# Hybrid decoder trunk: coefficient buffers moved by 960 bytes, the convolution norm's last gate ahead of its spread, two tiles and the squares of x made over the layer's end, gathers one a tile

## The chip, the cores and the metric

One core of one Trainium2 chip runs the whole program, two layers on 512 tokens, in one launch. The metric is the device time in microseconds.

## The reference, cut to what matters

```python
for l in range(DEPTH):                                   # DEPTH = 2, D = 1024, 512 tokens, fp32
    mod = silu(c) @ ada_w[l] + ada_b[l]
    sh1, sc1, g1, sh2, sc2, g2 = split(mod, 6)
    h = rms_norm(x, norm_mix_g[l]) * (1 + sc1) + sh1
    q, k, v, glu, gates = split(h @ w_in[l])             # 16 query heads, 4 key heads of 64
    attn = sliding_window_attention(rope(q), rope(k), v, sinks) @ w_o_attn
    u = ga * sigmoid(gb)
    u = silu(layer_norm(causal_conv31(u), conv_ln_g, conv_ln_b))
    merged = sigmoid(g_attn) * attn + sigmoid(g_conv) * (u @ w_o_conv)
    x = x + g1 * (merged @ w_out)
    h = rms_norm(x, norm_ffn_g[l]) * (1 + sc2) + sh2
    s = product_key_scores(h @ w_query, sub_keys)        # 8 heads, 2 x 128 keys
    ids, gate = top 16 of the pairs of the two halves' top 16, softmax
    x = x + g2 * sum(gate * gelu(u_tab[ids] . h) * v_tab[ids])
```

## The kernel before, in words

Every product with a weight matrix goes over a stream of tiles of 128 x 1024 numbers (512 KB), NT = 340 a layer: 28 input projections (4 glu, 2 keys, 2 values, 8 queries, 12 glu), attention gates and outputs (28 to 43), convolution gates 44 to 47 (I_CG), convolution outputs from 48, w_out at 60, queries of the retrieval at 68, then 128 tiles of the table u (I_U = 84) and 128 of the table v (I_W = 212). SP loads tile n into one of four slots of `raw` once tile n - 4 is used up; ACT rounds it to fp32r (`high`, L850), and DVE or POOL subtracts to get the low part in place (`w_low`, L1212; `u_low`, L1610; `weight_low`, L1672; POOL's `low`, L488). PE then makes 24 products a tile: high by high, high by low, low by high, over eight chunks of 128 features (`product`, L546 to L548; two tiles together in `first_pair`, L560 to L562; table v in `experts`, L804 to L806). Each engine's order is written out by hand, with counting semaphores between.

**A norm** (`norm`, twice a layer): ACT squares a chunk of x into one of two `sq` buffers (L880), PE adds over the features with four small products a chunk (`token_sums`, L578), ACT takes the root, DVE the inverse and a diagonal matrix (L1218, L1221), PE spreads it over the partitions (`spread`, L586), and DVE, ACT and DVE make each chunk of h, in high and low parts. The convolution's norm goes in the same way, with silu instead (L1041). There `spread` comes ahead of gate tile I_CG + 3, and ACT reads that gate out of its bank (`first_gate(3)`, L1015) only behind its eight silus; the first pair of the convolution's outputs needs that bank.

**The start.** SP issues the small inputs, ACT x and 16 rows of ada_w, then ACT makes silu of c and two sines of which DVE makes the arguments; DVE multiplies the rows with it (L1178). Tiles 0 and 1 are loaded, rounded by ACT at the head of a layer, and their low parts made by POOL.

**Retrieval.** Table u is multiplied densely for the last 384 tokens; for the first 128 POOL gathers rows (L507), one for each of 128 chosen experts of 128 tokens, into four slots, and DVE takes their dot product with h (`dot`, L1496); a slot is refilled once its dot is done (L519 to L523). While PE takes tiles 0 to 35 of u, DVE makes the top-k of the 4 token blocks, alone on its engine (L1533 to L1604), POOL makes the low parts, and ACT stops for one exp a block (`EXP_TILES`, L1095). From tile 36 (`U_ROUTE`) on DVE makes the low parts; between tiles 38 and 39 PE transposes the routing. From tile 40 on DVE makes one-hot matrices for 48 groups of 8 tokens (L1632, L1635), PE multiplies them (L778), and dots are shared out over the groups (`DOTS_BY_GROUP`); after the last group each of the last ten low parts has a dot behind it (L1640), then come any dots that are left (L1644). Table v starts with two `mix` (L1659) of what the first table left in memory (`cg`), a weight's low part and `mixed_low` (L1666); each tile's coefficients stand in `cf_hi` and `cf_lo`, four buffers each. DVE adds the gathered rows of v beside them (`weigh`, L1651).

At the layer's end DVE adds eight chunks to x (L1728) as PE transposes the sparse part (L812); after the last layer SP stores each chunk.

## Time and profile before

| | us |
|---|---|
| three runs | 3776.2, 3789.8, 3793.5; median 3789.8 |
| the profiled execution, its own time | 3782.4 |
| its span, first to last instruction | 3780.6 |
| PE busy | 3615.9 (96%) |
| DVE busy | 3099.5 (82%) |
| ACT busy | 1574.4 (42%) |
| POOL busy | 1381.1 (37%) |

The profile is one execution recorded by the hardware. PE is the matrix engine, DVE the vector engine, ACT the scalar engine, POOL GpSimd, SP the queue that issues most transfers. L12 is line 12 of the kernel before. A row of a timeline is: start in us from the span's start, duration in us, engine, line, operation, what it writes and reads, count, and in brackets how long the engine had been idle before it and what ended that. PE's instructions overlap, so a busy PE is not one at its best pace. An fp32 product stands as two instructions.

### The profile page before, as it was taken

The page shows a single profiled execution, that of the slowest core. Times are in us where ns is not written, and L with a number is a line of the kernel's source. Part 1 is how long each engine was busy: PE and PEld are TensorE (multiplying, and loading weights), DVE is VectorE, ACT ScalarE, POOL GpSimd, SP SyncE. Part 2 cuts the span into 40 slices and gives each one's busy share as a digit, 9 for nine tenths or more (in the row PEclk, how much of TensorE's full clock was granted, in tenths as well). Part 3 has the DMA queues.
Part 4 walks back from the last instruction along what each step waited for, and adds up shares of the span by engine and source line. Part 5 has one row for each costly group of instructions (what it writes and reads, how often), then busy time and mean ns, then how long its engine had stood idle before and what let it go on. Part 6 is the DMA issues. An engine that isn't in the chain of part 4 may idle for free.

```text
span 3780.6 us, 61655 instructions
## 1 busy us (share of the span) xinstructions
PE 3615.9 (96%) x19426; PEld 3325.2 (88%) x19426; DVE 3099.5 (82%) x6295; ACT 1574.4 (42%) x2321; POOL 1381.1 (37%) x1136
## 2 busy tenths in 40 slices
PE   5999899999999999999999998999999999999999
PEld 4766678989999999999987676889999999999999
DVE  6799765997888978888868995669978888788888
ACT  3474324434444533333345633244444554333332
POOL 0000002463555645454400000035645555545555
PEclk9999899999999999999999998989999999999999
DMA  4111253456999999999921111724579999999998
GB/s 178 62 56 56 67 215 119 133 175 204 317 335 346 289 350 342 339 339 342 330 87 62 51 67 58 255 95 140 177 228 331 356 322 301 353 333 345 350 336 283
DMA packets 408317, 862.51 MB, mean 228 GB/s; under 512 B 165488, under 2 KB 231024, under 8 KB 407664
## 3 DMA queue, kind: packets, MB, share of 16 engines
q1 hardware_dynamic: 294720, 528.08, 41.8%
q0 software_dynamic: 73728, 268.47, 20.2%
q10 hardware_dynamic: 39600, 62.93, 4.4%
q8 instruction: 100, 1.64, 0.2%
q14 instruction: 169, 1.38, 0.1%
HBM read 773.36 MB, written 85.98 MB: 227 GB/s over the span
## 4 chain that ended last, share of the span: by engine, by line
issue 47%; PE 34%; POOL 11%; DVE 4%; DMA 3%; ACT 0%; POOLq 0%; SPq 0%; DVEq 0%; ACTq 0%
PE ps L804 9%; PE ps L806 9%; PE ps L805 9%; POOL w_lo L488 7%; POOL gbuf L507 3%; PE ps L548 2%; PE ps L546 2%; PE ps L547 2%; POOL spare L522 2%; DMA raw<-stream 2%; PE ps L778 1%; DVE oneR L1635 1%; DVE gbuf L1496 1%; DVE oneL L1632 1%; DMA gbuf<-u_rows,ids_u 1%
## 5 line engine op out<-in xcount | busy, mean ns | idle before, releaser
L850 ACT CAST w_hi<-raw 128x1024 fp32r<-128x1024 f32 x680 | 715.3, 1055 | 910.7 <-DMA raw<-stream 864.2
L546 PE MATMUL ps<-h_hi,w_hi 128*128 128x384 f32 (+1 forms) x2944 | 1069.7, 363 | 25.6 <-POOL w_lo L488 16.3
L547 PE MATMUL ps<-h_lo,w_hi 128*128 128x384 f32 (+1 forms) x2944 | 1042.9, 354 | 0.0
L548 PE MATMUL ps<-h_hi,w_lo 128*128 128x384 f32 (+1 forms) x2944 | 1042.3, 354 | 0.0
L804 PE MATMUL ps<-cf_hi,w_hi 128*128 128x384 f32 x2048 | 697.2, 340 | 9.3 <-DVE cf_lo L1666 4.8
L806 PE MATMUL ps<-cf_hi,w_lo 128*128 128x384 f32 x2048 | 691.7, 338 | 0.0
L805 PE MATMUL ps<-cf_lo,w_hi 128*128 128x384 f32 x2048 | 687.1, 336 | 0.0
L522 POOL TENSOR_TENSOR spare<-spare 128x1 f32<-128x1 f32 x504 | 339.3, 673 | 901.5 <-DVE y_sp L1651 474.3
L546 PEld LDWEIGHTS ps<-h_hi,w_hi 128*128 128x128 f32 x2944 | 560.0, 190 | 79.2 <-POOL w_lo L488 18.1
L547 PEld LDWEIGHTS ps<-h_lo,w_hi 128*128 128x128 f32 x2944 | 559.8, 190 | 38.7 <-issue 5.8
L548 PEld LDWEIGHTS ps<-h_hi,w_lo 128*128 128x128 f32 x2944 | 558.8, 190 | 37.0
L488 POOL TENSOR_TENSOR w_lo<-raw,w_hi 128x1024 fp32r<-128x1024 f32 x108 | 288.6, 2678 | 332.3 <-ACT w_hi L850 332.0
L804 PEld LDWEIGHTS ps<-cf_hi,w_hi 128*128 128x128 f32 x2048 | 384.5, 188 | 12.3 <-DVE w_lo L1672 9.1
L507 POOL DMA_INDIRECT gbuf<-stream,ids_v x256 | 379.9, 1484 | 38.2 <-POOL spare L522 2.7
L507 POOL DMA_INDIRECT gbuf<-u_rows,ids_u x256 | 370.8, 1448 | 40.1 <-POOL spare L522 7.5
L805 PEld LDWEIGHTS ps<-cf_lo,w_hi 128*128 128x128 f32 x2048 | 384.5, 188 | 0.0
L806 PEld LDWEIGHTS ps<-cf_hi,w_lo 128*128 128x128 f32 x2048 | 383.9, 187 | 0.0
L499 POOL TENSOR_TENSOR spare<-spare 128x1 f32<-128x1 f32 x2 | 0.4, 193 | 1032.9 <-DVE w_lo L1212 1032.9
L1651 DVE SCALAR_TENSOR_TENSOR y_sp<-gbuf,a_sp,y_sp 128x1024 f32<-128x1024 f32 x256 | 327.1, 1278 | 5.2 <-DMA gbuf<-stream,ids_v 5.2
L1090 ACT ACTIVATE g_out<-ps 128x384 f32<-128x384 f32 x256 | 125.6, 491 | 490.9 <-PE ps L548 490.7
L1303 DVE SCALAR_TENSOR_TENSOR yT<-uT,lp,yT 128x512 f32<-128x512 f32 x480 | 327.6, 745 | 0.1
L1496 DVE CUSTOM_DVE_ANT_1 gbuf<-gbuf,h_tok 128x1024 f32<-128x1024 f32 x256 | 303.2, 1220 | 25.1 <-DMA gbuf<-u_rows,ids_u 25.0
(232 smaller groups left out, 4980.1 us busy)
## 6 DMA issues: line engine op xcount, KB each, us to landing
raw<-stream SPq DMA_DIRECT2D x680, 512.0 KB, 4.6
gelu_scratch<-g_out ACTq DMA_DIRECT2D x256, 192.0 KB
cg<-gelu_scratch SPq DMA_DIRECT2D x256, 192.0 KB, 5.9
c_scratch<-stage SPq DMA_DIRECT2D x64, 512.0 KB, 8.4
cg<-c_scratch SPq DMA_DIRECT2D x256, 128.0 KB, 4.9
qT<-ada SPq DMA_DIRECT2D x32, 512.0 KB, 6.0
cgate<-ada SPq DMA_DIRECT2D x32, 512.0 KB, 5.3
w_rows<-ada SPq DMA_DIRECT2D x32, 512.0 KB, 7.4
```

Source lines behind the costliest of these rows:

```text
L488: nc.gpsimd.tensor_tensor(w_lo[:, s], raw[:, s], w_hi[:, s].bitcast(F32), ALU.subtract).then_inc(lo_done, 1)
L507: nc.gpsimd.indirect_dma_start(out=gbuf[:, n % SLOTS], out_offset=None, in_=table, in_offset=bass.IndirectOffsetOnAxis(ap=ids[:, k:k + 1], ...
L522: nc.gpsimd.tensor_tensor(spare[:, 16:17], spare[:, 17:18], spare[:, 18:19], ALU.add).then_inc(room, 1)
L546: nc.tensor.matmul(ps[:, b, 0:n], wh, hi[:, c, t0:T], start=c == 0, stop=False)
L547: nc.tensor.matmul(ps[:, b, 0:n], wh, lo[:, c, t0:T], start=False, stop=False)
L548: mm = nc.tensor.matmul(ps[:, b, 0:n], wl, hi[:, c, t0:T], start=False, stop=c == C - 1)
L804: nc.tensor.matmul(ps[:, c, P:T], w_hi[:, s, c], cf_hi[s][:], start=first, stop=False)
L805: nc.tensor.matmul(ps[:, c, P:T], w_hi[:, s, c], cf_lo[s][:], start=False, stop=False)
L806: mm = nc.tensor.matmul(ps[:, c, P:T], w_lo[:, s, c], cf_hi[s][:], start=False, stop=last)
L850: nc.scalar.copy(w_hi[:, s], raw[:, s]).then_inc(hi_done, 1)
L1303: ins = nc.vector.scalar_tensor_tensor(out=yT[:, c], in0=uT[:, c, k:k + T], scalar=weight, in1=yT[:, c], op0=ALU.mult, op1=ALU.add)
L1496: nc.vector.tensor_tensor_reduce(out=row, in0=row, in1=h_tok[:, :, 0:P], scale=1.0, scalar=0.0, op0=ALU.mult, op1=ALU.add, accum_out=a_sp[ ...
```

## The change

- The buffers from `rstd` on begin 960 bytes later, and `cf_lo2` and `cf_lo3` are moved inside the space of h's low part. Widths stay.
- The squares of x for the mixer's norm get eight buffers of their own (over sq, hx, hs, sg). They and the rounding of the next layer's first two tiles come at the end of a layer, and ahead of the loop for layer 0. DVE adds the squares of chunks 4 to 7 into one, so that PE sums five sets and not eight, and DVE, not POOL, makes the low parts of tiles 0 and 1. The stream gets two more tiles at its end, for loads with no reader.
- SP issues x, the rows of ada and tiles 0 and 1 at the start.
- The convolution's gate tile I_CG + 3 is multiplied ahead of the spread; ACT copies its bank to `cgate` at once and takes the sigmoid there behind the silus.
- The exps come at tiles 8, 16, 24, 33; POOL's first four gathers come one a tile from tile 16; six dots come ahead of the routing's copies, and 104 are shared out over the groups.

Three new semaphores for the squares and one for the gate are left out below, as is unchanged code.

```diff
--- before.py
+++ after.py
@@ -47,9 +47,9 @@
...
 PART = NKEYS // PARTS
-EXP_TILES = (6, 14, 23, 32)
+EXP_TILES = (8, 16, 24, 33)
 SLOTS = 4
-GATHER_TILE = 18
+GATHER_TILE = 16
@@ -57,7 +57,7 @@
...
 ROW4 = PAIRS[1][0] * TOPK // 4 - PAIRS[1][0]
-DOTS_BY_GROUP = 118
+DOTS_FIRST, DOTS_BY_GROUP = 6, 104
@@ -202,6 +202,7 @@
...
         sinT = keep("sinT", [P, T])
+        cur[0] += 960
@@ -276,12 +277,13 @@
...
         cf_lo = [at("cf_lo0", rstd_base, [P, ND], F32R), at("cf_lo1", base + 67 * KB, [P, ND], F32R),
-                 at("cf_lo2", h_lo_base + 4 * KB, [P, ND], F32R), at("cf_lo3", h_lo_base + 6 * KB, [P, ND], F32R)]
+                 at("cf_lo2", h_lo_base + 4928, [P, ND], F32R), at("cf_lo3", h_lo_base + 6464, [P, ND], F32R)]
...
         gbuf = at("gbuf", sq_base, [P, SLOTS, D])
+        x_squares = at("x_squares", sq_base, [P, C, T])
@@ -399,7 +405,12 @@
...
             sp.dma_start(cact[:], c_d.broadcast_to([P, D])).then_inc(c_in, 16)
+            sp.dma_start(xT[:], x_d).then_inc(x_in, 16)
             sp.dma_start(params[:], params_d).then_inc(const_in, 16)
+            for n in range(ADA_1):
+                if n >= 12 and n % 2 == 0:
+                    sp.dma_start(raw[:, n // 2 - 6], stream[n // 2 - 6]).then_inc(loaded[n // 2 - 6], 16)
+                sp.dma_start(rows0[:, n], ada[n]).then_inc(ada_in[n // 4], 16)
@@ -421,7 +432,9 @@
...
-                with sp.Fori(0, 52 // 4) as r:
+                load(2, l * NT + 2)
+                load(3, l * NT + 3)
+                with sp.Fori(1, 52 // 4) as r:
@@ -469,6 +482,8 @@
...
                 w_loads(3, 0, 28, False)
+                load(0, l * NT + NT)
+                load(1, l * NT + NT + 1)
@@ -480,6 +495,7 @@
...
             nc.gpsimd.memset(spare[:, 15:20], 0.0).then_inc(lo_done, 4)
+            pool.wait_ge(lo_done, 4)
@@ -488,9 +504,6 @@
...
-                pool.wait_ge(lo_done, l * NT + 4)
-                for i in range(2):
-                    low(i, l * NT + i)
@@ -513,9 +526,8 @@
...
                     low(u % 4, l * NT + I_U + u)
-                    if u == GATHER_TILE:
-                        for n in range(SLOTS):
-                            gather(n)
+                    if GATHER_TILE <= u < GATHER_TILE + SLOTS:
+                        gather(u - GATHER_TILE)
@@ -572,11 +584,11 @@
...
-                def token_sums(b, c):
+                def token_sums(b, squares, first, last):
                     for tt in range(NB):
-                        mm = nc.tensor.matmul(ps[:, b, 2 * tt:2 * tt + 2], sq[:, c % 2, tt * P:(tt + 1) * P],
-                                              mean[:, 0:2], start=c + tt == 0, stop=c == C - 1 and tt == NB - 1)
+                        mm = nc.tensor.matmul(ps[:, b, 2 * tt:2 * tt + 2], squares[:, tt * P:(tt + 1) * P],
+                                              mean[:, 0:2], start=first and tt == 0, stop=last and tt == NB - 1)
@@ -587,13 +599,14 @@
...
-                def norm_sums(w):
-                    for c in range(C):
-                        pe.wait_ge(sq_done, (2 * l + w) * C + c + 1)
-                        token_sums(7 * w, c).then_inc(sq_used, 1)
-                    spread(7 - w, 3 * l + 2 * w)
-                norm_sums(0)
+                for c in range(5):
+                    if c < 4:
+                        pe.wait_ge(sqx_done, l * C + c + 1)
+                    else:
+                        pe.wait_ge(sqx_sum, 3 * l + 3)
+                    mm = token_sums(0, x_squares[:, c], c == 0, c == 4)
+                mm.then_inc(sqx_used, 1)
+                spread(7, 3 * l)
@@ -719,10 +732,9 @@
...
                     pe.wait_ge(ln_sq, l * C + c + 1)
-                    token_sums(6, c).then_inc(ln_mm, 1)
+                    token_sums(6, sq[:, c % 2], c == 0, c == C - 1).then_inc(ln_mm, 1)
+                proj(I_CG + 3, h_hi, h_lo)
                 spread(5, 3 * l + 1)
-                for i in range(I_CG + 3, I_CG + FIRST_GATES):
-                    proj(i, h_hi, h_lo)
@@ -730,7 +742,10 @@
...
                 proj_loop(I_OUT + 4, I_QRY, o_hi, o_lo)
-                norm_sums(1)
+                for c in range(C):
+                    pe.wait_ge(sq_done, l * C + c + 1)
+                    token_sums(7, sq[:, c % 2], c == 0, c == C - 1).then_inc(sq_used, 1)
+                spread(6, 3 * l + 2)
@@ -829,9 +844,6 @@
...
-            act.dma_start(xT[:], x_d).then_inc(x_in, 16)
-            for n in range(ADA_1):
-                act.dma_start(rows0[:, n], ada[n]).then_inc(ada_in[n // 4], 16)
@@ -839,8 +851,22 @@
...
             nc.scalar.copy(ident_r[:], ident).then_inc(id_r, 1)
+            def root_table():
+                nc.scalar.activation(spare[:, 30:31], eps, ACT.Sqrt)
+            def squares_of_x(c):
+                nc.scalar.activation(x_squares[:, c], xT[:, c], ACT.Square).then_inc(sqx_done, 1)
+            root_table()
+            act.wait_ge(x_in, 16)
+            for c in range(C):
+                squares_of_x(c)
             act.wait_ge(primed, 1)
-            act.wait_ge(x_in, 16)
+            for i in range(2):
+                act.wait_ge(loaded[i], 16)
+                nc.scalar.copy(w_hi[:, i], raw[:, i]).then_inc(hi_done, 1)
@@ -858,28 +884,13 @@
...
-                def root_table():
-                    nc.scalar.activation(spare[:, 30:31], eps, ACT.Sqrt)
...
-                def norm(w):
-                    root_table()
-                    for c in range(C):
-                        n = (2 * l + w) * C + c
-                        if w == 0:
-                            act.wait_ge(x_upd, l * C + c + 1)
-                        else:
-                            act.wait_ge(bank_read[c % 2], read_no(I_OUT + c))
-                        if c >= 2:
-                            act.wait_ge(sq_used, (2 * l + w) * C + c - 1)
-                        nc.scalar.activation(sq[:, c % 2], xT[:, c], ACT.Square).then_inc(sq_done, 1)
-                    act.wait_ge(sq_used, (2 * l + w) * C + C)
-                    token_root(7 * w)
+                def modulated(w):
@@ -891,9 +902,9 @@
...
-                high_at(0)
-                high_at(1)
-                norm(0)
+                act.wait_ge(sqx_used, l + 1)
+                token_root(0)
+                modulated(0)
@@ -1034,6 +1045,8 @@
...
                 token_root(6)
+                act.wait_ge(tile_done, l * NT + I_CG + 3 + 5)
+                nc.scalar.copy(cgate[:, 3], ps[:, 1]).then_inc(bank_read[1], 1)
@@ -1042,7 +1055,8 @@
...
                     nc.scalar.copy(n_hi[:, c], hs[:, c % 2]).then_inc(ln_hi, 1)
-                first_gate(3)
+                act.wait_ge(bank_read[1], read_no(I_CG + 3))
+                nc.scalar.activation(cgate[:, 3], cgate[:, 3], ACT.Sigmoid).then_inc(late_gate, 1)
@@ -1059,7 +1073,15 @@
...
                         act.dma_start(keys[:], keys_d[ll]).then_inc(key_in, 16)
-                norm(1)
+                root_table()
+                for c in range(C):
+                    act.wait_ge(bank_read[c % 2], read_no(I_OUT + c))
+                    if c >= 2:
+                        act.wait_ge(sq_used, l * C + c - 1)
+                    nc.scalar.activation(sq[:, c % 2], xT[:, c], ACT.Square).then_inc(sq_done, 1)
+                act.wait_ge(sq_used, (l + 1) * C)
+                token_root(7)
+                modulated(1)
@@ -1139,6 +1161,12 @@
...
                         high_at(I_W + NKEYS - 4 + s + 2)
+                high_at(NT)
+                root_table()
+                for c in range(C):
+                    act.wait_ge(x_upd, (l + 1) * C + c + 1)
+                    squares_of_x(c)
+                high_at(NT + 1)
@@ -1185,11 +1213,28 @@
...
             parameters(slice(0, 1))
+            def sum_squares(counted):
+                dve.wait_ge(sqx_done, (counted + 1) * C)
+                nc.vector.tensor_tensor(x_squares[:, 4], x_squares[:, 4], x_squares[:, 5], ALU.add).then_inc(sqx_sum, 1)
+                nc.vector.tensor_tensor(x_squares[:, 6], x_squares[:, 6], x_squares[:, 7], ALU.add).then_inc(sqx_sum, 1)
+                dve.wait_ge(sqx_sum, 3 * counted + 2)
+                nc.vector.tensor_tensor(x_squares[:, 4], x_squares[:, 4], x_squares[:, 6], ALU.add).then_inc(sqx_sum, 1)
+            def first_low(i):
+                dve.wait_ge(hi_done, i + 1)
+                nc.vector.tensor_tensor(w_lo[:, i], raw[:, i], w_hi[:, i].bitcast(F32), ALU.subtract).then_inc(lo_done, 1)
...
                 modulate(rows0[:, n], mv[:, C + n:C + n + 1])
+                if n == 7:
+                    sum_squares(0)
+                if n >= ADA_1 - 2:
+                    first_low(n - ADA_1 + 2)
@@ -1346,7 +1391,6 @@
...
-                dve.wait_ge(lo_done, l * NT + 2 + 4)
@@ -1432,6 +1476,8 @@
...
                         dve.wait_ge(bank_read[m % 2], read_no(I_CG + m))
+                        if m == 3:
+                            dve.wait_ge(late_gate, l + 1)
@@ -1616,6 +1662,8 @@
...
                 dve.wait_ge(h_ev, 2 * l + 2)
+                for _ in range(DOTS_FIRST):
+                    dot()
@@ -1635,7 +1683,7 @@
...
                     last_one.then_inc(lr_done, 1)
-                    while dots[0] < (g + 1) * DOTS_BY_GROUP // GROUPS:
+                    while dots[0] < DOTS_FIRST + (g + 1) * DOTS_BY_GROUP // GROUPS:
@@ -1722,12 +1770,14 @@
...
                 prepare(l + 1)
+                w_low(NT)
...
                                                    in1=xT[:, c], op0=ALU.mult, op1=ALU.add).then_inc(x_upd, 1)
-                dve.wait_ge(x_upd, (l + 2) * C)
+                sum_squares(l + 1)
+                w_low(NT + 1)
@@ -1761,7 +1811,7 @@
...
                   a["peer_v"][l].reshape(P, NKEYS, C, P).transpose(1, 0, 2, 3)]
-    stream = np.concatenate(tiles)
+    stream = np.concatenate(tiles + [tiles[0][:2]])
```

## Rows read from the trace of the kernel before

**Rows 1.** The page: engines over the whole span.

```profile
PE 3615.9 (96%) x19426; PEld 3325.2 (88%) x19426; DVE 3099.5 (82%) x6295; ACT 1574.4 (42%) x2321; POOL 1381.1 (37%) x1136
```

**Rows 2.** Groups by line, PE: busy us, mean ns | idle us before, releasers.

```profile
L778 PE MATMUL ps<-oneR,oneL 128*128 128x128 f32 x1536 | 190.1, 277 | 17.0 <-DVE oneR L1635 16.8
```

**Rows 3.** Timeline of the start: ACT, DVE and PE.

```profile
23.92 1.06 ACT L836 ACTIVATE cact<-cact 128x1024 f32<-128x1024 f32 x1
...
30.15 1.22 DVE L1178 CUSTOM_DVE_ANT_0 rows<-rows,cact 128x1024 f32<-128x1024 f32 x1
...
53.36 0.20 DVE L1218 RECIPROCAL rs<-rs 128x8 f32<-128x8 f32 x1
...
59.17 0.77 PE L560 MATMUL ps<-h_hi,w_hi 128*128 128x512 f32 x1 [3.15 <-DVE h_lo L1230]
```

**Rows 4.** Transfers from 0 to 60 us, in 40 slices of 1.5 us.

```profile
GB/s 0 177 287 365 340 422 361 418 422 415 424 418 421 418 423 421 415 421 426 415 423 412 426 415 366 19 0 0 0 0 0 0 0 0 0 0 0 0 5 0
DMA packets 3602, 14.21 MB, mean 237 GB/s; under 512 B 400, under 2 KB 400, under 8 KB 3472
```

**Rows 5.** Timeline at the two layer ends: PE and DVE.

```profile
1912.14 11.00 PE L578 MATMUL ps<-con,sq 128*128 128x2 f32 x64 [0.98 <-issue]
...
3772.54 5.36 DVE L1728 SCALAR_TENSOR_TENSOR xT<-ps,md,xT 128x512 f32<-128x512 f32 x8 [1.43 <-PE ps L812]
```

**Rows 6.** Timeline of PE at the convolution's norm and the second norm.

```profile
446.79 9.77 PE L578 MATMUL ps<-con,sq 128*128 128x2 f32 x48 [1.04 <-ACT sq L1021]
...
473.86 0.76 PE L560 MATMUL ps<-n_hi,w_hi 128*128 128x512 f32 x1 [8.01 <-ACT cgate L1015]
...
487.63 0.49 PE L546 MATMUL ps<-n_hi,w_hi 128*128 128x512 f32 x1 [0.35 <-DVE hx L1445]
...
604.88 0.80 PE L560 MATMUL ps<-h_hi,w_hi 128*128 128x512 f32 x1 [3.06 <-DVE h_lo L1230]
...
617.48 1.16 PE L743 MATMUL ps<-keys,qk 128*128 128x128 f32 x8
```

**Rows 7.** Timeline of the routing: PE, DVE and POOL.

```profile
779.94 0.44 PE L546 MATMUL ps<-h_hi,w_hi 128*128 128x384 f32 x1 [2.79 <-POOL w_lo L488]
...
796.43 7.43 DVE L1600 TENSOR_TENSOR routed<-t,esum 128x128 f32<-128x128 f32 x1
...
796.70 7.00 POOL L488 TENSOR_TENSOR w_lo<-raw,w_hi 128x1024 fp32r<-128x1024 f32 x3
...
799.11 0.69 PE L546 MATMUL ps<-h_hi,w_hi 128*128 128x384 f32 x1 [5.92 <-POOL w_lo L488]
...
873.74 0.44 PE L546 MATMUL ps<-h_hi,w_hi 128*128 128x384 f32 x1 [2.09 <-DVE w_lo L1610]
...
888.50 1.49 DVE L1621 COPY ijg<-ps 128x384 f32<-128x384 f32 x3 [12.54 <-PE ps L790]
```

**Rows 8.** Stretch of tiles 0-35: PE, PEld, DVE, ACT, POOL, clock, DMA, GB/s.

```profile
710.00:872.00 162.00, 152.94 (x869) 151.47 (x868) 158.50 (x457) 68.61 (x87) 103.11 (x38) 0.98 0.55 169
```

**Rows 9.** Timeline from the last dot to the second table: DVE and PE.

```profile
1355.43 1.22 DVE L1496 CUSTOM_DVE_ANT_1 gbuf<-gbuf,h_tok 128x1024 f32<-128x1024 f32 x1
...
1364.14 0.42 DVE L1659 TENSOR_TENSOR coef<-cg 128x256 f32<-128x256 f32 x1 [4.68 <-DMA cg<-gelu_scratch]
...
1366.51 0.44 PE L804 MATMUL ps<-cf_hi,w_hi 128*128 128x384 f32 x1 [2.50 <-DVE cf_lo L1666]
```

**Rows 10.** DMA issues, 1318 to 1364 us: count, median us to landing.

```profile
gbuf<-u_rows,ids_u POOLq DMA_INDIRECT x9, 7.8
```

**Rows 11.** Stretches, PE alone: length, busy (count), clock, DMA share, GB/s.

```profile
1400.00:1640.00 240.00, 240.00 (x1368) 1.00 1.00 346
711.00:769.00 58.00, 58.00 (x336) 1.00 0.55 162
...
79.00:95.00 16.00, 16.00 (x72) 1.00 0.29 99
347.00:368.00 21.00, 21.00 (x92) 1.00 0.24 76
```

4 lines of the change are left out of this document (added).

## The prediction, before the change was run

> **What bounds the kernel now.** The page's engine table comes first: TensorE (PE) is busy for 96% of the span, so time can only come from PE's remaining idle time and from the pace at which its instructions follow one another [rows 1]. Next, the groups by line for PE with the idle time before each, both layers summed: among them 17.0 us before the one-hot products, waiting for DVE [rows 2]. Then the timelines around those places, read for what ended each wait; last the starts of PE's instructions, to see their spacing. Times below are of layer 0; layer 1 repeats the pattern, and I double.
>
> **The start.** ACT issues x and 16 rows of ada itself, its queue fills up, and so its first activation runs only at 23.92 us, and with it silu, both tables, DVE's row products and PE's first real product, at 59.17, come late [rows 3]. The transfers are not what it waits for at the end: 14.21 MB move at about 420 GB/s and are done by 37.5 us [rows 4]. The change puts all issues on SP, in the order pos, constants, c, x, parameters, rows, with two tiles put between the last rows. Ahead of the last row then stand 13.1 of those 14.2 MB, which lands it near 36 us; SP's issues are 22 in a row, and nothing else waits on that queue but tiles 2 and 3, wanted after 50 us. ACT no longer issues, so silu and both tables are through by about 18 us, before the first four rows are in (about 18.6). DVE then does 16 products of 1.2 us, now with 2 us of added sums and two low parts that POOL had made, of the same 128 x 1024 elements and so 1.2 us each. The last group of four rows decides: 36 + 4 x 1.2 + 2.4 = 43.2 us, where DVE's reciprocal stood at 53.36. From it to PE's first product everything stays (59.17 - 53.36 = 5.8 us), so PE starts at 49 and not at 59. **-10 us** (bounds -6, if the single queue drains as slowly as in its first 5 us, and -12).
>
> **Between the layers.** The last tile's x updates run 5.36 us on DVE (the row is layer 1's), then the token sums hold PE for 11.00 us from 1912.14: eight sets, 1.4 us each on average [rows 5]. After the change there are five sets. ACT squares each chunk behind DVE's update (0.67 us a piece), with nothing to wait for, and is done at about 1912.8; DVE's three additions of 0.7 us end at 1915; PE is still in its first four sets then, so the fifth finds its data. Five average sets would take 6.9 us; the first ones, straight behind busy PE work, should be the quick ones, so I take 5.5 instead of 11.0: **-5.5 us** (bounds -4 and -7). The two weight tiles made here cost nothing: DVE stands still before the first update, and the second tile lies beside PE's sums; without that cover they would cost 1.2 us each. POOL loses this work and nobody waits for it. Once only, at the very end of the program, the same squares, sums and low part run with no reader: DVE ends some 4 us after its last update (3772.54 + 5.36 = 3777.9), the last output landed 2.7 us after it, with the span's end, **+1 us**.
>
> **The last convolution gate.** Before, PE's sums end at 456.6, then come spread, gate tile 3 (to 465.9), and an idle wait of 8.01 us for a bank that ACT frees only after its whole silu chain; the first pair is through at 487.6 [rows 6]. After, the tile runs straight behind the sums (24 products at 0.23 us and the first of them at the lower clock, to about 464), ACT copies the bank out, spread takes 1.2 us (four fp32 products at full clock, as the row of L743), and the first pair follows chunk by chunk as in the second norm: 3.06 us of wait and 12.6 us of work [rows 6]. End at about 481: 6.6 us earlier. What is late next is the weight tile behind the pair: its high part stands on ACT behind silus and the moved sigmoid with its table load, so I give back 0.6. **-12 us** for two layers (bounds -8 and -15). The DVE wait added for that sigmoid comes four tiles later and costs nothing.
>
> **Routing, gathers one a tile.** PE loses 2.79 us where ACT waits for the second exp, and 5.92 us where POOL issues four gathers in a row; both go, since exp comes two tiles later, and one gather fits beside one low part in the 4.16 us of a tile (24 products at 173.6 ns). But PE cannot keep this: at tile 36 the low parts pass to DVE, which comes there only when its routing chain ends, and PE waits for it already today, 2.09 us, to 873.74 [rows 7]. That chain is DVE's alone: DVE is busy for 158.50 us of the 162 up to there [rows 8]. So of the 8.7 us only what the chain itself gets shorter is kept. It loses 7.1 us in one place, an operation of 0.29 us that took 7.43 behind three low parts which POOL made up in a row after its gathers; spread out, these parts of 2.3 us will hold up other operations instead [rows 7]. I take 4 us kept: **-8 us** for two layers (bounds -17 and +9, the latter if the 7.1 us stay in another form and two more operations a layer are held up).
>
> **Dots.** Six dots move into DVE's 12.54 us wait for the transposes [rows 7], where they are free: the first four find their rows, two wait for a refill and end about 2 us before the wait does. The groups then carry 104 instead of 118. Of 17 us before the one-hot products [rows 2] I take **-6 us** (bounds 0 and -12). But 6 + 104 + 10 (one with each remaining low part) is 120: eight dots stay over, and they stand behind the last low part, ahead of the first coefficients. Today the last dot ends at 1356.6, DVE's second mix starts at 1364.14, when its data has landed, and PE starts the second table at 1366.5 [rows 9]. Eight dots on four slots are two rounds; a gather lands 7.8 us (median) after its issue in this stretch [rows 10], so they end near 1371 to 1373, and the mix follows. **+16 us** for two layers (bounds 0, if rows land fast, and +26).
>
> **Addresses.** The 960 bytes and the two offsets move all eight coefficient buffers, and with them o and n, to 448 modulo 512 (by the allocation's sums; now cf_hi, cf_lo0, cf_lo1, o and n stand at 0, cf_lo2 and cf_lo3 at 128, h at 128). Four stretches in which PE never waits give the spacing of its instructions, each as the stretch plus one instruction's own length over their count [rows 11]: coefficients, 384 columns, 240.34 / 1368 = 175.7 ns; h, 384 columns, 58.33 / 336 = 173.6; h, 512 columns, 16.4 / 72 = 227.8; o, 512 columns, 21.4 / 92 = 232.5. So streams that start at 0 are slower than those at 128, by 2.1 and 4.7 ns. No row shows 448. Bounds: downward the pace of h (2.1 x 6144 + 4.7 x 1152 = 18 us less), upward the coefficients as far above h as o is (2.6 x 6144 = 16 us more). I take the pace of h, because 0 is the only start seen slow, and all eight buffers leave it: **-18 us**. The Trainium skill, page "SBUF — State Buffer", section "SBUF: two separate sides", says that TensorE has ports of its own and waits for nobody, so an address would change nothing: by it this term is 0 and the sum 18 us higher. The two paces speak against it, if nothing but the address parts them. It is the first rival.
>
> **The sum.** -10 - 5.5 + 1 - 12 - 8 - 6 + 16 - 18 = -42.5. The profiled execution took 3782.4 us (span 3780.6): 3740. It is below the median of the three runs shown (3789.8); the mean of all four is 3785.5, so I add 3: **3743 us**.
>
> **Rivals.**
> 1. **The address gives nothing.** For it: the weights' loads and the moving data share an engine, and 448 is seen nowhere; against it: the two paces in the rows. 3743 + 18 = 3761 us. Chance 0.24.
> 2. **The leftover dots cost nothing,** because their rows have landed and the second mix waits for cg in any case (1364.14). Against it: a refill needs the dot before. 3743 - 16 = 3727 us. Chance 0.08.
> 3. **They cost double,** with the first weigh waiting for v rows whose gathers stand behind the eight dots: 3759 us. Chance 0.05.
> 4. **Slower: POOL's parts and gathers stretch the routing chain.** Its 36 low parts a layer now come evenly, while DVE is in two-input operations; if half of them hold up operations that go free today, at 2.3 us each, the chain grows by 42 us a layer, all of it paid at tile 36: 3743 + 8 + 84 = 3835 us. It decides from some 13 such hits a layer (3809 us). Against it: half of the chain is single-input searches, which lose nothing. Chance 0.05.
>
> The forecast itself has 0.58. **The numbers.** A measurement of this kernel tells about 0.5% (19 us) from no change. Forecast: 0.56 faster, 0.02 same; rival 1: 0.17 and 0.07; rival 2: 0.08 faster; rival 3: 0.04 and 0.01; rival 4: 0.01 same, 0.04 slower. Together 0.85, 0.11 and 0.04. The range 3722 to 3768 holds rivals 1 to 3 and the forecast with its bounds of 10 to 15 us.
>
> **What would show it.** First product of PE near 49 us. Token sums between the layers x40 in about 5.5 us. No wait on L1015's gate; a 3 us wait before the first pair instead. The two idle times of 2.79 and 5.92 gone, and that before tile 36 up from 2.09 to 6 or 7 us. PE's wait before the second table up from 2.50 to about 10 us, with eight dots behind the last low part. Coefficient products 173.5 ns apart. The forecast is wrong if that spacing stays, if tile 36 starts later against the second norm than now, or if the wait at the second table stays under 4 us.

## The result, and the profile after

The changed kernel takes 3750.0 us (median of 4 runs, 3743.4 to 3753.8), the kernel before 3785.7 beside it on the same chip (4 runs, 3776.2 to 3793.5): ratio 0.9905, 95% interval 0.9875 to 0.9934, that is 36 us or 0.95% less. The profiled run has a span of 3741.6 us against 3780.6.

The page's engine row of the changed kernel (before: [rows 1]):

```profile
PE 3580.1 (96%) x19378; PEld 3297.4 (88%) x19378; DVE 3098.4 (83%) x6310; ACT 1577.9 (42%) x2333; POOL 1390.0 (37%) x1132
```

PE has 48 instructions less (three sets of sums, twice), and 36 us less of busy time. The groups by line on PE show where its waits went (busy, mean ns | idle before, releasers; both layers):

```profile
L558 PE MATMUL ps<-h_hi,w_hi 128*128 128x384 f32 (+1 forms) x2944 | 1067.7, 363 | 21.4 <-DVE w_lo L1656 16.7 <-POOL w_lo L504 4.5
L819 PE MATMUL ps<-cf_hi,w_hi 128*128 128x384 f32 x2048 | 692.2, 338 | 38.0 <-DVE cf_lo L1714 29.4 <-DVE w_lo L1720 8.4
L793 PE MATMUL ps<-oneR,oneL 128*128 128x128 f32 x1536 | 187.9, 275 | 2.1 <-DVE oneR L1683 2.1
```

The coefficient products in the kernel before:

```profile
L804 PE MATMUL ps<-cf_hi,w_hi 128*128 128x384 f32 x2048 | 697.2, 340 | 9.3 <-DVE cf_lo L1666 4.8 <-DVE w_lo L1672 4.5
```

The wait before the one-hot products, 17.0 us before [rows 2], is 2.1; in its place the coefficient products wait 38.0 us and not 9.3, 29.4 of them for the first coefficient's low part of each layer. L558 was L546 before, L572 was L560, L819 was L804, L793 was L778.

The same in stages, from start to start of PE's instructions (us, layer 0 / layer 1; each is the difference of two start times in the timelines; a spread is the group of products by which PE copies a norm's factors over the partitions):

| stage | before | after | change, both |
|---|---|---|---|
| start, to the first spread | 53.9 | 44.4 | -9.5 |
| first norm's spread to second norm's | 545.8 / 543.4 | 538.5 / 537.7 | -13.0 |
| to table u's first product (queries) | 110.6 / 111.9 | 111.9 / 110.7 | +0.1 |
| to tile 40 (routing) | 186.8 / 187.5 | 180.2 / 182.6 | -11.5 |
| to tile 117 (groups) | 420.9 / 418.3 | 409.4 / 408.8 | -21.0 |
| to the second table's first product | 48.5 / 48.3 | 60.5 / 61.0 | +24.7 |
| second table | 544.2 / 543.0 | 539.9 / 541.1 | -6.2 |
| layer 0's end, to the next spread | 13.3 | 9.6 | -3.7 |
| last product to the span's end | 4.1 | 5.5 | +1.4 |

Together -38.7, the spans' difference but for rounding.

**Start.** Timeline of the changed kernel, ACT, DVE, PE:

```profile
7.33 1.06 ACT L848 ACTIVATE cact<-cact 128x1024 f32<-128x1024 f32 x1 [5.29 <-DMA cact<-c_in]
...
18.39 1.23 DVE L1206 CUSTOM_DVE_ANT_0 rows<-rows,cact 128x1024 f32<-128x1024 f32 x1 [1.50 <-DMA rows<-ada]
...
43.83 0.20 DVE L1263 RECIPROCAL rs<-rs 128x8 f32<-128x8 f32 x1
...
49.49 0.79 PE L572 MATMUL ps<-h_hi,w_hi 128*128 128x512 f32 x1 [3.00 <-DVE h_lo L1275]
```

Silu runs at 7.33 instead of 23.92 and the row products start at 18.39, when their rows land; the reciprocal is 9.5 us earlier, and so is all behind it [rows 3].

**Gate.** PE at the convolution's norm:

```profile
435.91 9.67 PE L590 MATMUL ps<-con,sq 128*128 128x2 f32 x48 [1.04 <-ACT sq L1032]
445.44 0.77 PE L558 MATMUL ps<-h_hi,w_hi 128*128 128x512 f32 x1
...
453.34 1.05 PE L598 MATMUL ps<-rstd,con 128*128 128x128 f32 x8
457.77 0.76 PE L572 MATMUL ps<-n_hi,w_hi 128*128 128x512 f32 x1 [3.38 <-DVE n_lo L1462]
...
471.62 0.50 PE L558 MATMUL ps<-n_hi,w_hi 128*128 128x512 f32 x1 [1.28 <-DVE hx L1491]
```

From the sums after their wait to the tile behind the pair it is 35.71 us (471.62 - 435.91), before 40.84 (487.63 - 446.79 [rows 6]). The 8.01 us wait for ACT's bank is gone; 3.38 us stand in its place, and 1.28 (2.43 in layer 1) behind the pair, where it had been 0.35. In layer 1 the same stretch takes 35.46 us, before 40.84: 10.5 us in both layers.

**Routing.** PE before tile 36 in both layers, and the one place where POOL still holds it up:

```profile
780.77 0.45 PE L558 MATMUL ps<-h_hi,w_hi 128*128 128x384 f32 x1 [2.23 <-POOL w_lo L504]
...
853.25 0.69 PE L558 MATMUL ps<-h_hi,w_hi 128*128 128x384 f32 x1 [4.08 <-DVE w_lo L1656]
...
2703.73 0.69 PE L558 MATMUL ps<-h_hi,w_hi 128*128 128x384 f32 x1 [8.22 <-DVE w_lo L1656]
```

2.79 and 5.92 [rows 7] have become 2.23 and nothing, and the wait for DVE's routing chain (the top-k work that it has to end before it makes low parts) has grown from 2.09 to 4.08 in layer 0 and 8.22 in layer 1.

**From the first table to the second.** DVE, then PE:

```profile
1326.42 1.23 DVE L1542 CUSTOM_DVE_ANT_1 gbuf<-gbuf,h_tok 128x1024 f32<-128x1024 f32 x1 [1.81 <-DMA gbuf<-u_rows,ids_u]
...
1331.70 1.22 DVE L1542 CUSTOM_DVE_ANT_1 gbuf<-gbuf,h_tok 128x1024 f32<-128x1024 f32 x1 [4.04 <-DMA gbuf<-u_rows,ids_u]
...
1340.76 1.22 DVE L1542 CUSTOM_DVE_ANT_1 gbuf<-gbuf,h_tok 128x1024 f32<-128x1024 f32 x1 [1.77 <-DMA gbuf<-u_rows,ids_u]
...
1341.91 0.42 DVE L1707 TENSOR_TENSOR coef<-cg 128x256 f32<-128x256 f32 x1
...
1344.81 0.68 PE L819 MATMUL ps<-cf_hi,w_hi 128*128 128x384 f32 x1 [14.46 <-DVE cf_lo L1714]
```

The eight leftover dots end at 1341.9; six of them wait for the row of a slot that was refilled only after an earlier dot, three of which are shown. The mix then starts without a wait (before, it waited for cg [rows 9]). PE's wait is 14.46 us, where it was 2.50.

**Layer end.** Five sets of sums, where there were eight [rows 5]:

```profile
1885.96 7.38 PE L590 MATMUL ps<-con,x_squares 128*128 128x2 f32 x40 [0.83 <-ACT x_squares L860]
```

### The profile page after: what moved, and what is told of

It is laid out like the page before. It is cut to its first block, busy times and chain, and to the rows that moved or that the text cites. A ratio compares the mean times of both kernels' runs of the same rounds, so it can differ in the third digit from the quotient of the medians.

```text
span 3741.6 us, 61584 instructions
## 1 busy us (share of the span) xinstructions
PE 3580.1 (96%) x19378; PEld 3297.4 (88%) x19378; DVE 3098.4 (83%) x6310; ACT 1577.9 (42%) x2333; POOL 1390.0 (37%) x1132
## 4 chain that ended last, share of the span: by engine, by line
PE 40%; issue 35%; DVE 11%; POOL 10%; DMA 2%; ACT 2%; POOLq 0%; DVEq 0%; SPq 0%; ACTq 0%
PE ps L819 9%; PE ps L820 8%; PE ps L821 8%; POOL gbuf L520 4%; PE ps L558 4%; PE ps L560 4%; PE ps L559 4%; POOL w_lo L504 3%; POOL spare L534 3%; DMA raw<-stream 1%; DVE yT L1348 1%; PE ps L793 1%; DVE i L1554 1%; DVE eq L1625 1%; PE ps L590 1%
## 5 line engine op out<-in xcount | busy, mean ns | idle before, releaser
L558 PE MATMUL ps<-h_hi,w_hi 128*128 128x384 f32 (+1 forms) x2944 | 1067.7, 363 | 21.4 <-DVE w_lo L1656 16.7
L560 PE MATMUL ps<-h_hi,w_lo 128*128 128x384 f32 (+1 forms) x2944 | 1041.3, 354 | 0.0
L819 PE MATMUL ps<-cf_hi,w_hi 128*128 128x384 f32 x2048 | 692.2, 338 | 38.0 <-DVE cf_lo L1714 29.4
L534 POOL TENSOR_TENSOR spare<-spare 128x1 f32<-128x1 f32 x504 | 359.9, 714 | 884.3 <-DVE a_sp L1542 442.3
L558 PEld LDWEIGHTS ps<-h_hi,w_hi 128*128 128x128 f32 x2944 | 558.4, 190 | 74.4 <-DVE w_lo L1656 17.8
L560 PEld LDWEIGHTS ps<-h_hi,w_lo 128*128 128x128 f32 x2944 | 557.0, 189 | 38.2
L819 PEld LDWEIGHTS ps<-cf_hi,w_hi 128*128 128x128 f32 x2048 | 386.1, 189 | 42.6 <-DVE w_lo L1720 42.1
L512 POOL TENSOR_TENSOR spare<-spare 128x1 f32<-128x1 f32 x2 | 0.4, 192 | 1022.7 <-DVE w_lo L1257 1022.7
L520 POOL DMA_INDIRECT gbuf<-u_rows,ids_u x256 | 358.0, 1398 | 39.1 <-POOL spare L534 9.9
```

Source lines behind the costliest of these rows:

```text
L520: nc.gpsimd.indirect_dma_start(out=gbuf[:, n % SLOTS], out_offset=None, in_=table, in_offset=bass.IndirectOffsetOnAxis(ap=ids[:, k:k + 1], ...
L534: nc.gpsimd.tensor_tensor(spare[:, 16:17], spare[:, 17:18], spare[:, 18:19], ALU.add).then_inc(room, 1)
L558: nc.tensor.matmul(ps[:, b, 0:n], wh, hi[:, c, t0:T], start=c == 0, stop=False)
L560: mm = nc.tensor.matmul(ps[:, b, 0:n], wl, hi[:, c, t0:T], start=False, stop=c == C - 1)
L819: nc.tensor.matmul(ps[:, c, P:T], w_hi[:, s, c], cf_hi[s][:], start=first, stop=False)
```

## The experiments

Medians stand beside the kernel before, run on the same chip in the same hour (3783.2 to 3785.6); "against the changed kernel" compares with its 3750.0, which was measured at another time, so that a difference of some 3 us says nothing. The ratios of experiments 1, 2 and 12 and of the 256 bytes in 5 have intervals clear of the changed kernel's (0.9875 to 0.9934); the others overlap it, and there the stages of the one profiled execution have to carry the reading. Every run but the second is an edit of the changed kernel.

**1 and 2. The addresses, taken back, and alone.**

```diff
-        cur[0] += 960
...
-                 at("cf_lo2", h_lo_base + 4928, [P, ND], F32R), at("cf_lo3", h_lo_base + 6464, [P, ND], F32R)]
+                 at("cf_lo2", h_lo_base + 4 * KB, [P, ND], F32R), at("cf_lo3", h_lo_base + 6 * KB, [P, ND], F32R)]
```

The second run is the kernel before with the opposite of this and nothing else.

> The changed kernel with the 960 bytes and the two offsets taken back (coefficient buffers, o and n again at 0, two low parts at 128, modulo 512). Theory (the start address sets the pace of the products): coefficient products go from 173.0 back to about 175.4 ns apart, o's and n's to 232, while the waits inside the second table, which grew when the pace rose, shrink again by some 5 us a layer; net about +8 us against the changed kernel, near 3758. As the prediction had it: +18, 3768. Rival (the pace came from something else in the change): spacing stays at 173.0, time stays at 3750.

> The kernel before with only the 960 bytes and the two offsets. Theory (the start address sets the pace, but part of what it gives is lost in waits for low parts of the weights inside the second table): spacing 173.0 ns for coefficients, second table about 540 to 541 us long instead of 544, and -6 to -8 us in all, near 3778. As the prediction had it: -18, 3768. Rival (the pace came from something else in the change): spacing 175.4, time 3786.

Measured: taken back 3767.6 us (5 runs, 3764.8 to 3771.6; ratio to before 0.9955, interval 0.994 to 0.9969), alone 3767.9 us (8 runs, 3757.8 to 3780.0; ratio 0.9957, 0.994 to 0.9974). The address is worth 17.6 us from the one side (3767.6 - 3750.0) and 17.3 from the other (3785.2 - 3767.9). Stretches of 200 us in the second table and of 40 us with o, in which PE never waits: the changed kernel, then the kernel with the addresses back (columns as in [rows 8]):

```profile
1400.00:1600.00 200.00, 200.00 (x1156) 200.00 (x1155) 168.74 (x253) 69.25 (x96) 104.06 (x95) 1.00 1.02 351
528.00:568.00 40.00, 40.00 (x176) 32.81 (x176) 28.37 (x44) 11.46 (x13) 5.01 (x3) 1.00 0.81 303
```

```profile
1400.00:1600.00 200.00, 200.00 (x1140) 200.00 (x1139) 167.70 (x250) 68.97 (x95) 109.90 (x100) 1.00 1.01 344
530.00:570.00 40.00, 40.00 (x173) 32.15 (x173) 28.21 (x44) 11.47 (x13) 5.00 (x3) 1.00 0.81 297
```

Worked as in the prediction, 200.34 / 1156 = 173.3 ns against 200.34 / 1140 = 175.7, at the same clock and the same DMA load. The kernel with the addresses alone has x1156 in 200 us, too. My own expectation, +8 and -7, was half of what came. I had taken the 6.2 us of the second table's row for the whole; but the changed kernel loses more in waits inside that table, whatever the addresses: what the intervals of over 0.2 us between its products have beyond 173.5 ns adds up, over both layers, to 7.4 us before, 15.8 in the changed kernel and still 12.8 with the addresses back. With the table's start and end read in the two runs that differ by the address alone, it is 546.0 / 546.6 back against 539.9 / 541.1: 11.6 us. The other way round, the addresses alone take it from 544.2 / 543.0 to 536.9 / 539.2: 11.1. In the stage of the gate it is 540.7 / 539.0 against 538.5 / 537.7, 3.5 us, which fits what o and n should give (4 ns x 1152 = 4.6), but other runs with o and n at 448 differ by as much in that stage. The rival (something else sets the pace) is out: the spacing follows the address in both directions, and the products with h, which no run moves, stay at 173.4 to 173.6 ns (384 columns) in all 14 profiled executions.

**3. The dots as before.**

```diff
-DOTS_FIRST, DOTS_BY_GROUP = 6, 104
+DOTS_FIRST, DOTS_BY_GROUP = 0, 118
```

> The changed kernel with the dots as before (0 first, 118 with the groups, 10 with the last low parts). Theory (the groups' waits and the eight leftover dots cancel): tile 117 of the first table comes 9 to 11 us a layer later, the wait before the second table falls from 14.5 to about 2.5 us a layer, time stays within 5 us of 3750. As the prediction had it (the dots' edits cost 10 us in all): 3740. Rival (the shorter groups are worth more than the wait, since later work hangs on them): 3760 or more.

Measured: 3736.9 us (5 runs, 3727.3 to 3747.6; ratio 0.9876, 0.9856 to 0.9897), 13 us less than the changed kernel. PE's groups:

```profile
L819 PE MATMUL ps<-cf_hi,w_hi 128*128 128x384 f32 x2048 | 693.1, 338 | 10.4 <-DVE w_lo L1720 5.8 <-DVE cf_lo L1714 4.6
L793 PE MATMUL ps<-oneR,oneL 128*128 128x128 f32 x1536 | 189.8, 277 | 16.0 <-DVE oneR L1683 12.9 <-issue 3.0
```

38.0 goes to 10.4 and 2.1 to 16.0. By stages the groups take 416.3 / 421.2 us (+19.3) and the way to the second table 48.3 / 48.3 (-24.9): -5.6, the profiled spans differ by 6.6. The medians say 13, and the two ratios' intervals overlap a little (0.9856 to 0.9897 against 0.9875 to 0.9934). That this part of the change costs time is likely by that, its size is not settled; experiments 4 and 10, in which every execution is quicker than every one of the changed kernel, bear out that the leftover dots cost. The groups' gain is no chance of one profile: in the three runs with the dots as before they take 415.6 to 421.2 us a layer, in the nine with 104 dots 408.5 to 410.8.

**4. The leftover dots spread over the last low parts.**

```diff
                     lows += 1
                     dot()
+                    if lows > NKEYS - 8:
+                        dot()
```

> The changed kernel with the eight leftover dots moved forward, a second one behind each of the last seven or eight low parts of the first table. Theory (DVE has about 12 us of idle time between the last ten low parts, and rows land in time for two dots a tile): the wait before the second table falls from 14.5 to 3 or 4 us a layer, PE loses at most 2 us a layer in the last tiles, so about -20 us, near 3730. Rival (the rows of the gathers are what is late, a slot's refill takes longer than two dots a tile allow, and the low parts then wait behind dots): the same 11 us a layer come back as waits of PE in tiles 120 to 127, time stays near 3750.

Measured: 3734.4 us (4 runs, 3730.6 to 3737.1; ratio 0.9865, 0.9848 to 0.9882). From tile 117 to the second table it takes 55.1 / 52.9 us instead of 60.5 / 61.0, so -13.5. PE's timeline there:

```profile
1330.52 0.44 PE L558 MATMUL ps<-h_hi,w_hi 128*128 128x384 f32 x1 [3.57 <-DVE w_lo L1656]
...
1341.44 0.44 PE L819 MATMUL ps<-cf_hi,w_hi 128*128 128x384 f32 x1 [2.31 <-DVE cf_lo L1716]
```

The wait before the table falls as expected, and about 4 to 7 us a layer come back before the last tiles, more than the 2 I allowed: there DVE waits for rows, and a low part stands behind it. The rival's mechanism is there, at about half of its size (6.8 and 4.6 us of 11).

**5 to 7. Other places for the same buffers:** 256, 64 and 128 modulo 512.

```diff
-        cur[0] += 960
+        cur[0] += 256
...
-                 at("cf_lo2", h_lo_base + 4928, [P, ND], F32R), at("cf_lo3", h_lo_base + 6464, [P, ND], F32R)]
+                 at("cf_lo2", h_lo_base + 4224, [P, ND], F32R), at("cf_lo3", h_lo_base + 5760, [P, ND], F32R)]
```

The other two have 64 with 4544 and 6080, and 128 with 4096 and 6144, in the same places.

> The changed kernel with all eight coefficient buffers, o and n at 256 modulo 512 instead of 448. Theory A (only a start at 0 modulo 512 is slow): spacing 173.0 ns, o's products of 512 columns at 227 to 229, time near 3750. Theory B (what counts is the distance from the weights, which stand at 128 modulo 512, or from a 256-byte boundary): spacing 175 ns or more, time 3765 or more. Theory C (any move in the rest of the memory changes it, and 448 was luck): some third value.

> The same at 64 modulo 512. Theory A (only 0 is slow): spacing 173.0 ns, time near 3750, as with 256 and 448. Theory B (starts at odd multiples of 64 are the quick ones, at multiples of 128 or 256 the slow ones): 173.0 here, too, but 175 with 256. Theory C (448 was luck): some third value.

> The changed kernel with the eight coefficient buffers, o and n at 128 modulo 512, where h and both weight buffers stand. 0, 64 and 256 have each given 175.4 to 176 ns, 448 gives 173.0. Theory D (quick is a stream whose start has the weights' place modulo 512, as h has, and 448 is quick for another reason): 173.0 for the coefficients and 227 for o's and n's 512 columns, where 448 leaves them at 226 to 231: time 3746 to 3750. Theory E (448 alone is quick for these buffers, and h's pace has a reason of its own, such as its start past the first 512 bytes of a chunk): 175.5 to 176 ns, 3765.

Stretches without a wait at 256, 64 and 128, in this order:

```profile
1640.00:1840.00 200.00, 200.00 (x1138) 200.00 (x1137) 168.73 (x252) 68.76 (x95) 95.81 (x98) 1.00 1.00 340
527.00:567.00 40.00, 40.00 (x173) 32.17 (x172) 28.54 (x44) 11.39 (x13) 5.00 (x3) 1.00 0.82 301
```

```profile
1660.00:1860.00 200.00, 200.00 (x1134) 200.00 (x1133) 168.72 (x253) 69.74 (x96) 98.88 (x95) 1.00 1.01 338
531.00:571.00 40.00, 40.00 (x173) 32.08 (x172) 28.91 (x45) 10.98 (x13) 4.57 (x3) 1.00 0.81 296
```

```profile
1655.00:1855.00 200.00, 200.00 (x1155) 200.00 (x1155) 173.13 (x259) 70.58 (x97) 109.33 (x98) 1.00 1.00 341
528.00:553.00 25.00, 25.00 (x112) 20.67 (x111) 19.49 (x31) 5.78 (x6) 0.00 (x0) 1.00 0.91 346
```

| start modulo 512 | coefficients, ns | o, 512 columns, ns | time, us (runs) |
|---|---|---|---|
| 0 (two low parts at 128) | 175.7 | 233.5 | 3767.6 (5) |
| 64 | 176.7 | 233.5 | 3763.8 (4) |
| 128 | 173.5 | 226.8 | 3748.1 (5) |
| 256 | 176.0 | 233.5 | 3768.6 (4) |
| 448 | 173.3 | 229.5 | 3750.0 (4) |

One product more or less in a stretch of o is 1.3 ns (2 ns at 128, whose stretch is shorter). The means of all intervals between starts say the same: o 227.0 at 128, 229.1 to 229.6 at 448, 232.8 to 233.3 at 0, 64 and 256, and n with it.

Theory A falls with the first two: 0 is not the only slow start. That odd multiples of 64 are quick falls with 64, which is slow; the distance from the weights, the other theory B, lives on as theory D. 128, where h and both weight buffers stand, is quick for both lengths; 448 is quick for 384 columns and in between for 512. So theory D (quick is a start at the weights' place) came true at the one place tried, but 448 does not meet its condition. In the profiled runs the pattern is regular: at 256 every one of the 24 positions in a tile stands at 176 ns, at 448 and 128 every one at 173 or 174, while before a tile mixed 170 to 182. Why an address changes the pace, and what sets 448 apart, stays open; 192, 320 and 384, and another place for the weights, weren't tried.

**8. The gathers and exps back.**

```diff
-EXP_TILES = (8, 16, 24, 33)
+EXP_TILES = (6, 14, 23, 32)
-GATHER_TILE = 16
+GATHER_TILE = 18
...
-                    if GATHER_TILE <= u < GATHER_TILE + SLOTS:
-                        gather(u - GATHER_TILE)
+                    if u == GATHER_TILE:
+                        for n in range(SLOTS):
+                            gather(n)
```

> The changed kernel with the four gathers in a row at tile 18 again and the exponentials at tiles 6, 14, 23 and 32. Theory (PE's waits of 2.8 and 5.9 us come back in each layer, and the one before tile 36 shrinks from 4 to 8 us to about 2): tile 36 stands 3 to 5 us a layer later against the second norm, +8 us in all, near 3758. Rival (DVE's routing chain alone sets tile 36, so that PE's earlier waits only come out of the last one): within 2 us of 3750.

Measured: 3762.5 us (5 runs, 3757.4 to 3765.2; ratio 0.9939, 0.9926 to 0.9952), 12.5 more than the changed kernel. PE's waits in its routing:

```profile
765.04 0.69 PE L559 MATMUL ps<-h_hi,w_hi 128*128 128x384 f32 x1 [2.73 <-POOL w_lo L504]
784.20 0.69 PE L559 MATMUL ps<-h_hi,w_hi 128*128 128x384 f32 x1 [4.83 <-POOL w_lo L504]
...
859.46 0.44 PE L559 MATMUL ps<-h_hi,w_hi 128*128 128x384 f32 x1 [2.09 <-DVE w_lo L1657]
```

And in DVE's chain:

```profile
781.51 7.43 DVE L1647 TENSOR_TENSOR routed<-t,esum 128x128 f32<-128x128 f32 x1
```

All three waits are back, and so is DVE's operation of 7.43 us [rows 7]; in the changed kernel no operation of that chain takes over 4.42. To tile 36 it costs 5.5 and 2.3 us (164.0 and 163.4 from the table's start, against 158.5 and 161.1), 7.7 as expected; from there to tile 40 another 1.7 a layer, which I hadn't counted. The rival is out: tile 36 comes at 163.4 to 164.1 us in all layers of the three runs with the gathers in a row, at 158.4 to 161.1 in all of the eleven others, so DVE's chain itself is shorter. Which part of that is the gathers' and which the exps' isn't shown, as both went back together. Runs with equal code here differ, though: from table u's start to tile 40 they took 180.1 to 184.0 us, which is over half of what a layer gains.

**9. The gate back behind the spread.**

```diff
-                proj(I_CG + 3, h_hi, h_lo)
                 spread(5, 3 * l + 1)
+                proj(I_CG + 3, h_hi, h_lo)
...
-                act.wait_ge(tile_done, l * NT + I_CG + 3 + 5)
-                nc.scalar.copy(cgate[:, 3], ps[:, 1]).then_inc(bank_read[1], 1)
...
-                act.wait_ge(bank_read[1], read_no(I_CG + 3))
-                nc.scalar.activation(cgate[:, 3], cgate[:, 3], ACT.Sigmoid).then_inc(late_gate, 1)
+                first_gate(3)
...
-                        if m == 3:
-                            dve.wait_ge(late_gate, l + 1)
```

> The changed kernel with the convolution norm's last gate behind the spread again, ended by ACT behind its silus. Theory (the 8 us wait for ACT's bank comes back, against 3.4 us before the first pair and 1 to 2.4 us behind it now): +6 to +7 us a layer, +13 in all, near 3763. Rival (what the earlier gate gives is lost again in later waits for low parts that the same silus hold up): the second norm's sums come less than 3 us a layer later, and the time stays within 6 us of 3750.

Measured: 3757.2 us (6 runs, 3752.7 to 3777.4; ratio 0.9941, 0.992 to 0.9961), +7.1. The two waits, in layer 0 and 1:

```profile
462.34 0.76 PE L572 MATMUL ps<-n_hi,w_hi 128*128 128x512 f32 x1 [8.18 <-ACT cgate L1026]
...
2322.05 0.77 PE L572 MATMUL ps<-n_hi,w_hi 128*128 128x512 f32 x1 [7.90 <-ACT cgate L1026]
```

From norm to norm 541.6 / 541.6 us, 3.1 and 3.9 more than the changed kernel. But that stage is long, and parts of it that the edit doesn't touch differ between runs: up to the sums before the gate it was 0.6 and 1.8 us shorter here, behind the gate's stretch 1.4 shorter and 0.4 longer. The gate's own stretch, from the start of these sums to the tile behind the pair, takes 40.75 / 40.68 us, where the changed kernel has 35.71 / 35.46: 10.3 us. It takes 35.4 to 36.4 in every layer of the eleven runs with the gate ahead of the spread, and 40.7 to 40.9 in the three with it behind. So the gate is worth 10 us where it works, nearer to the theory's 13 than to the rival. The whole time tells it only roughly: 7 us by the medians, 14 by the ratios (0.9941 against 0.9905, with intervals that overlap), since two of the six executions took 3769 and 3777. Before, the same stage took 545.8 / 543.4: of the 13.0 us gained there 10.5 are the gate's stretch (40.84 us in both layers before).

**10. 112 dots in the groups, none left over.**

```diff
-DOTS_FIRST, DOTS_BY_GROUP = 6, 104
+DOTS_FIRST, DOTS_BY_GROUP = 6, 112
```

> The changed kernel with 112 dots in the groups instead of 104, so that none is left over. Theory (the eight dots cost 12 us a layer ahead of the second table, and fewer in the groups, where 14 of them made 10 us, so eight make 5 or 6): second table's wait 14.5 to 2.5, tile 117 some 5 us later, -6 us a layer, -12 in all, near 3738. Rival (the groups have no room for more than 104, each dot costs its full 1.2 us and the row it waits for): 3750.

Measured: 3732.7 us (4 runs, 3726.0 to 3737.5; ratio 0.9869, 0.9851 to 0.9887), -17.4. PE's groups:

```profile
L819 PE MATMUL ps<-cf_hi,w_hi 128*128 128x384 f32 x2048 | 691.3, 338 | 9.4 <-DVE w_lo L1720 4.8 <-DVE cf_lo L1714 4.6
L793 PE MATMUL ps<-oneR,oneL 128*128 128x128 f32 x1536 | 188.8, 276 | 12.4 <-DVE oneR L1683 9.7 <-issue 2.7
```

Against the changed kernel the groups take 12.7 us more (415.3 / 415.5), the way to the second table (48.3 / 48.3) 25 less: 12 of the 17 us. The same eight dots cost about 0.8 us each in the groups and 1.6 each where they were left.

**11. The leftover dots behind the first mixes.**

```diff
-                while dots[0] < P:
-                    dot()
...
                 mixed_low(0, 0)
+                while dots[0] < P:
+                    dot()
+                dve.wait_ge(row_used, l * 2 * P + P + SLOTS)
```

> The changed kernel with the eight leftover dots behind the first two mixes, the first low part of the second table's weights and of its coefficients, instead of ahead of them. Theory (PE can then do its first coefficient tile beside them, 4.2 us, and DVE's 2.9 us ahead of the first product no longer come after them): the wait before the second table falls from 14.5 to 3 to 5 us, a new one of 4 to 8 us stands before its second tile, -4 to -7 us a layer, near 3739. Rival (all of it comes back before the second tile, as the mixes then come late once more): 3750.

Measured: 3745.2 us (5 runs, 3741.6 to 3753.2; ratio 0.9905, 0.9888 to 0.9923): the changed kernel's ratio. PE at the table's start:

```profile
1333.20 0.68 PE L819 MATMUL ps<-cf_hi,w_hi 128*128 128x384 f32 x1 [2.63 <-DVE cf_lo L1712]
...
1354.03 0.69 PE L819 MATMUL ps<-cf_hi,w_hi 128*128 128x384 f32 x1 [14.94 <-DVE w_lo L1718]
```

The last added line keeps DVE from clearing `y_sp`, which lies over the features that the dots read, before they are through. The wait moved one tile on and kept its length: behind the dots still stand a mix, a `weigh` and the second tile's low parts. The rival was right, by another way than it named.

**12. 112 dots and 128 modulo 512 together.**

```diff
-DOTS_FIRST, DOTS_BY_GROUP = 6, 104
+DOTS_FIRST, DOTS_BY_GROUP = 6, 112
...
-        cur[0] += 960
+        cur[0] += 128
```

cf_lo2 and cf_lo3 stand at h_lo_base + 4096 and + 6144.

> The changed kernel with 112 dots in the groups and the coefficient buffers, o and n at 128 modulo 512. Theory (the two are independent: 112 dots gave about 17 us, and 128 takes o's and n's 512 columns to 227 ns): o's and n's stretch 1 to 3 us a layer shorter than with 448, coefficients at 173.0, wait before the second table 2.3, time 3730 to 3733. Rival (with 128 the second table loses more in waits for low parts, 12.8 us in one layer of the run with 128 alone): 3735 to 3740.

Measured: 3728.3 us (4 runs, 3723.8 to 3733.5; ratio 0.9855, 0.9836 to 0.9874). It is the fastest of all, 57 us below the kernel before beside it and 22 below the changed one; against run 10 its 4 us are within the intervals. That is a little below the expected 3730 to 3733, and the rival (3735 to 3740) is out. A stretch of o's products in it, x178 in 40 us where 448 gave x176:

```profile
2368.00:2408.00 40.00, 40.00 (x178) 33.14 (x177) 28.07 (x44) 11.46 (x13) 4.99 (x3) 1.00 0.81 300
```

## Why the prediction was right, and where its terms were off

The time (3743 forecast, 3750 measured) came out, partly by luck: terms were off on both sides and made up for each other.

| term | forecast | in the stages | by undoing it alone |
|---|---|---|---|
| start | -10 | -9.5 | not undone |
| between the layers | -5.5 | -3.7 | not undone |
| end | +1 | +1.4 | not undone |
| gate | -12 | -13.0 with o's and n's place, -10.5 in its own stretch | -10.3 in its own stretch |
| routing | -8 | -11.5 | -12.5 |
| dots in the groups | -6 | -21.0 | -19 (stages) |
| eight leftover dots | +16 | +24.7 | +25 (stages) |
| the two together | +10 | +3.7 | +6 to +13 |
| addresses | -18 | -6.2 in the second table | -17.6, -17.3 |

- **Start.** Each step came: silu once c has landed (7.3), row products from 18.4 (18.6 forecast), reciprocal at 43.8 (43.2), first product at 49.5 (49).
- **Layer end.** "The first ones should be the quick ones, so I take 5.5" didn't hold in this execution: x40 took 7.38 us, 1.48 a set, and the first of them waited 0.83 for ACT's squares. It is 1.8 us off. What was left out is the clock: over the twelve runs with five sets x40 took 5.39 us at a granted clock of 0.84 (experiment 3) to 7.85 at 0.56 (experiment 4), 7.38 at 0.60 here, and length times clock is 4.4 to 4.5 us each time. The 5.5 us came in some of them; which clock a run gets there is not explained.
- **Gate.** Mechanism as forecast, with a 3.38 us wait in place of 8.01. In its own stretch it gained 10.5 us, and lost 10.3 when undone alone: 12 was a little too much, within the bounds. Mis-sized is the give-back behind the pair, 0.6 forecast: that wait went from 0.35 to 1.28 and 2.43. The rest of the stage's 13.0 lies outside the stretch and isn't the gate's.
- **Routing.** The wait before tile 36 was to grow to 6 or 7 us and stood at 4.08 and 8.22; to tile 36 the gain was 4.9 and 3.0, 8 as forecast. Behind it come 1.7 and 1.9 us that the prediction didn't look for.
- **Dots.** Both terms were too small: the groups' waits went almost wholly (17.0 to 2.1, and I had taken 6 of 17), and the leftover dots raised the wait from 2.50 to 14.46 and not to 10. The second failed in "they end near 1371 to 1373", 7 to 9 us behind PE's end of the first table (1366.51 - 2.50 = 1364.0); they ended at 1341.9, 11.6 behind it (1344.81 - 14.46 = 1330.35). Two rounds of 7.8 us from the dot before them would be 15.6; they took 19.6, since rows landed one after the other. Rival 3 had this as its size (+32 for double; +24.7 came). Their sum cost 4 to 13 us against 10 forecast. By experiment 3 this part of the change was better left out, and by 10 its idea was right with eight dots more in the groups.
- **Addresses.** Forecast and measured agree within 1 us. The first rival (0 us) is out: 17 us hang on the address. The page of the Trainium skill that the prediction weighed ("SBUF — State Buffer", section "SBUF: two separate sides") says that TensorE never waits on anyone at its ports; it speaks of contention between engines and not of addresses, and that "an address would change nothing" was the prediction's step from it, which the 17 us do not bear out. But the ground I gave, that "0 is the only start seen slow" and would be the odd one, was wrong: 64 and 256 are as slow. Had the kernel moved by 256 bytes, the same argument would have said -18, and the run gave nothing. Nor do o and n reach h's pace at 448: 229.5 ns against 227.8. I was right by luck, at a place where I had no row.
- **POOL's parts and gathers** (rival 4) stretched nothing: tile 40 comes earlier in both layers.

## What to carry to other kernels

A buffer's start address is a parameter of the product's pace: read the spacing of instructions in stretches without waits, one stream against another, and if they differ move the slow one to where the quick one and the weights stand, and measure. Work taken from one stage of an engine has to be put somewhere: count the pieces that are left (6 + 104 + 10 of 128) and price them by the stage where they end up, each with the latency of what feeds it. And two kernels that differ in many parts can't be read for one part by one stage's length: here the second table's 6 us hid 12 of the address's, because other waits in it had grown.
